# First expert's rows by one-hot products on chip, routing on turned raw rows, and one instruction section for routing and experts

## The reference

```python
h = h + g1 * (mix_x @ w_out)
t = rmsnorm(h, norm_mlp_w) * (1 + sc2) + sh2          # h is (512, 1024)
logits = t @ w_router + b_router                       # 32 experts
top_vals, top_idx = lax.top_k(logits, 4)
weights = jax.nn.softmax(top_vals)
# every expert e, on the tokens that chose it:
gate, up = jnp.split(t[rows] @ w_gu[e] + b_gu[e], 2, axis=-1)
act = (up + 1) * min(gate, 7) * sigmoid(1.702 * min(gate, 7))
y[rows] += weight * (act @ w_down[e] + b_down[e])
h = h + g2 * y
```

## Time and profile before

| what | us |
|---|---|
| median of 3 runs | 2255.71 (2254.8 to 2259.87) |
| the profiled execution's own time | 2238.22 |
| its span, first to last instruction | 2236.4 |
| PE busy | 2151.9 (96%) |
| DVE busy | 839.2 (38%) |
| ACT busy | 465.4 (21%) |
| POOL busy | 217.1 (10%) |

### The profile page before, as it was taken

The page is one execution under the profiler, slowest core; times in us unless marked ns, Lnnn a source line. Parts: engine busy times, 40 slices in busy tenths (PEclk is TensorE's granted clock), DMA queues, the critical chain, the costliest instruction groups (busy, mean ns, idle before and its releaser), DMA issues.

```text
span 2236.4 us, 34362 instructions
## 1 busy us (share of the span) xinstructions
PE 2151.9 (96%) x14207; PEld 891.3 (40%) x14207; DVE 839.2 (38%) x1585; ACT 465.4 (21%) x863; POOL 217.1 (10%) x268
## 2 busy tenths in 40 slices
PE   5999896999999999999999998999999999999998
PEld 2434542333333333333333334484445444444443
DVE  1142536823323233232332456311475022565633
ACT  2030322101111011110111012110144021654630
POOL 1000002111111111111111312000000000000000
PEclk9999997999999999999999999999999999999999
DMA  9957128999999999999999997322210221112210
GB/s 372 352 199 280 48 89 336 409 420 422 420 419 421 420 415 423 421 421 422 421 417 423 420 421 286 136 95 87 75 57 1 75 85 57 62 51 94 75 38 38
DMA packets 107105, 565.97 MB, mean 253 GB/s; under 512 B 17290, under 2 KB 29367, under 8 KB 73219
## 3 DMA queue, kind: packets, MB, share of 16 engines
q1 hardware_dynamic: 84086, 512.93, 57.0%
q0 software_dynamic: 19728, 50.02, 6.3%
q10 hardware_dynamic: 3228, 2.17, 0.3%
HBM read 545.61 MB, written 37.62 MB: 261 GB/s over the span
## 4 chain that ended last, share of the span: by engine, by line
PE 80%; DVE 2%; DMA 2%; ACT 1%; issue 0%; POOL 0%; ACTq 0%; POOLq 0%; DVEq 0%; SPq 0%
PE ps L2099 29%; PE ps L2069 10%; PE ps L379 9%; PE ps L3220 5%; PE ps L3315 5%; PE ps L3233 5%; PE ps L2077 5%; PE ps L3258 4%; PE ps L3246 2%; DMA ring<-in_w_gu 1%; PE ps L2915 1%; PE ps L2906 1%; PE ps L2615 1%; PE ps L2659 1%; PE ps L2617 1%; PE ps L2899 1%
## 5 line engine op out<-in xcount | busy, mean ns | idle before, releaser
L2099 PE MATMUL ps<-ring,xeT 128*32 128x512 f32 x6144 | 671.1, 596 | 3.7 <-DMA ring<-in_w_gu 3.3
L2099 PEld LDWEIGHTS ps<-ring,xeT 128*32 128x32 f32 x6144 | 197.2, 110 | 449.9 <-issue 445.5
L2069 PE MATMUL ps<-ring,mT 128*32 128x512 f32 x2048 | 266.5, 592 | 0.0
L1784 ACT ACTIVATE mT<-mT 128x768 f32<-128x768 f32 x32 | 27.0, 843 | 851.7 <-DVE mT L1848 851.6
L1848 DVE TENSOR_TENSOR mT<-ps,spread_bias 128x768 f32<-128x768 f32 x32 | 30.6, 957 | 435.0 <-PE ps L2099 434.9
L2077 PE MATMUL ps<-ring,mT 128*32 128x256 f32 x2048 | 157.4, 379 | 0.0
L2077 PEld LDWEIGHTS ps<-ring,mT 128*32 128x32 f32 x2048 | 66.6, 110 | 153.2 <-issue 153.2
L3220 PE MATMUL ps<-hT_late,ring 128*128 128x512 f32 x256 | 111.9, 597 | 0.5 <-issue 0.5
L3233 PE MATMUL ps<-hT_late,ring 128*128 128x512 f32 x256 | 110.5, 592 | 0.0
L379 PE MATMUL ps<-hT_late,ring 128*128 128x512 f32 x256 | 110.4, 593 | 0.0
L3315 PE MATMUL ps<-ring,mT 128*128 128x512 f32 x256 | 110.2, 592 | 0.0
(11 more groups left out here) (435 smaller groups left out, 2231.0 us busy)
## 6 DMA issues: line engine op xcount, KB each, us to landing
ring<-in_w_gu SPq DMA_DIRECT2D x128, 2048.0 KB, 10.7
ring<-in_w_down SPq DMA_DIRECT2D x128, 1024.0 KB, 11.6
y_scratch<-zeros POOLq DMA_DIRECT2D x1, 20352.0 KB, 101.3
ring<-in_even_w_in SPq DMA_DIRECT2D x18, 1024.0 KB, 9.1
ring<-in_w_ada SPq DMA_DIRECT2D x32, 512.0 KB, 9.6
ring<-in_odd_w_in SPq DMA_DIRECT2D x32, 512.0 KB, 5.4
ring<-in_w_ada SPq DMA_DIRECT2D x8, 1024.0 KB, 18.6
ring<-in_w_in SPq DMA_DIRECT2D x8, 1024.0 KB, 20.6
```

The source lines that it names most:

```text
L2069: mm = nc.tensor.matmul(quad(b, 2 * q + n), acted(k, q, src), w[:, kk, n * BANK:(n + 1) * BANK], start=first, stop=last)
L2099: mm = nc.tensor.matmul(quad(q, c), left(q), part_columns(w, c), start=start, stop=stop)
```

## The change

The normalised rows `xnt` and their modulated turned copy are no longer made for the routing. PE turns the raw rows `res` as soon as each half is added (its wait is now `res_ready`, half by half), and ACT and DVE copy four turned tiles each in one instruction (`turned`). The scale moves into the router's weights: POOL multiplies `w_router` by it once (`w_scaled`). The shift becomes one row of 32 numbers that PE works out once (`shift`, `shifts`) and DVE adds to the bias; the reciprocal root multiplies the logits (`scalar_tensor_tensor` in `logits`). In PE's list `turn(3)` goes ahead of the ranks of blocks 0 to 2, and on DVE the last steps are reordered.

Expert 0's rows are made on chip. DVE writes `first_sel`, for each token block a 128 by 96 one-hot of expert 0's places times the reciprocal root, and PE multiplies the raw rows by it: for each of 8 k-tiles, four products of 128 by 128 (every second column of `res`) and 128 by 96, added in PSUM. ACT scales and shifts out of PSUM into `xeT`. The gather of expert 0, its transposing and the three rounds of row numbers stay in the program. Round 0 of the row numbers on PE comes behind all these products, rounds 1 and 2 come behind k-steps 1 and 5 of expert 0's gate and up product, and the turning of the biases behind k-step 3.

The end of the routing section and the start of the expert section are gone as a meeting of all engines. SP waits for the last `member_ready` in its place, and no longer for the first gather. The diff without changes of indentation, cut to its core:

```diff
             def _(pool):
                 posm_zero.on(nc.gpsimd.memset(posm[:], 0.0))
+                pool.wait_ge(stream.ready[slot], landed)
+                w_scaled_ready.on(nc.gpsimd.tensor_tensor(w_scaled, w_raw, mod2[:, KD:, 0:1].to_broadcast([P, KD, E]), ALU.mult))
...
-                    for k in range(4):
-                        ins = nc.scalar.activation(hT2[:, k, t * P:(t + 1) * P], ps[:, j.bank, k * P:(k + 1) * P], ACT.Identity,
-                                                   bias=mod2[:, k, 0:1], scale=mod2[:, KD + k, 0:1])
-                    j.empty(ins)
+                    j.empty(nc.scalar.activation(hT2[:, 0:4, t * P:(t + 1) * P], bank(j.bank).rearrange("p (k n) -> p k n", k=4),
+                                                 ACT.Copy))
...
-                    xn2_ready.on(nc.vector.tensor_scalar(xnt[:, t, :], res[:, t, :], at, None, ALU.mult))
...
+                    j.empty(nc.vector.tensor_copy(hT2[:, 4:KD, t * P:(t + 1) * P], bank(j.bank).rearrange("p (k n) -> p k n", k=4)))
...
+                    n2_mean.wait(dve)
+                    j.empty(nc.vector.scalar_tensor_tensor(out=logit[:, t, :], in0=ps[:, j.bank, t * E:(t + 1) * E],
+                                                           scalar=stat[:, 4 + t:5 + t], in1=brb, op0=ALU.mult, op1=ALU.add))
...
                 output(3)
                 logits(2)
-                choose(2)
-                normalise(3)
-                modulate(3)
+                pick(2)
+                turned(3)
+                mean(3)
+                mark_members(2)
                 router_part(3)
+                inverse(3)
                 logits(3)
                 choose(3)
...
                 def turn(t):
-                    pe.wait_ge(xn2_ready.sem, t + 1)
                     for b, j in enumerate(j_h2[t]):
+                        pe.wait_ge(res_ready.sem, 2 * t + b + 1)
...
+                def shift():
+                    j_shift.open(pe)
+                    for k in range(KD):
+                        mm = nc.tensor.matmul(ps[QUAD * (k % 4):QUAD * (k % 4 + 1), j_shift.bank, NT * E:NT * E + 2], w_router[:, k, :],
+                                              mod2[:, k, :], start=k < 4, stop=k >= 4)
+                    j_shift.done(mm)
...
                 logits(2)
+                turn(3)
                 pe.wait_ge(route.sem, 2)
                 j_rank.open(pe)
                 for t in range(3):
                     ranks(t)
-                turn(3)
                 router_part(3)
...
-        with nc.Block() as block:
             @block.sync
             def _(sp):
+                member_ready.wait(sp)
                 bgu_loaded.on(sp.dma_start(bgu, A["b_gu"][0]), 16)
...
-                sp.wait_ge(M.gathered, 48)
...
-                act.wait_ge(M.xT_done, 1)
-                act_modulate(act, M)
+                for j in range(KD):
+                    act.wait_ge(first_turned.sem, rows_turned + min(j // 3 * 3 + 3, KD))
+                    nc.scalar.activation(xeT[:, j, 0:CAP], first_rows(j), ACT.Identity,
+                                         bias=modx[:, j:j + 1], scale=modx[:, KD + j:KD + j + 1]).then_inc(M.xeT_read, 1)
...
+                j_rank.emptied_for(dve)
+                for t in range(NT):
+                    first_chosen.on(nc.vector.tensor_scalar(first_sel[:, t, :], places, posm[:, t, 0:1],
+                                                            stat[:, 4 + t:5 + t], ALU.is_equal, ALU.mult))
                 split_places(list_step, posm[:, :, 0:2], place[:, :, 0:2], third_of[:, :, 0:2])
...
-                for e in range(3):
-                    pe.wait_ge(M.onehot_ready, e + 1)
...
+                first_chosen.wait(pe)
+                for j in range(KD):
...
+                    at = j // 2 * 2 * P + j % 2
+                    for t in range(NT):
+                        mm = nc.tensor.matmul(first_rows(j), res[:, t, at:at + 2 * P - 1:2],
+                                              first_sel[:, t, :], start=t == 0, stop=t == NT - 1)
+                    first_turned.on(mm)
...
+                        if first and k in (1, 5):
+                            own_ids(1 + k // 4)
+                        if first and k == 3:
+                            turn_biases()
...
+                own_ids(0)
                 block_step(0, 0, 0, True, opening=True)
```

More of the change, by code:

```diff
@@ L1407, in _ @@
                 w_router = take(pe)
+                shift()
+                w_scaled_ready.wait(pe)
                 router_part(0)
                 output(2, range(4))
+                shifts()
                 logits(0)
@@ L1650, in build @@
-        j_dw = [psum.job(i, "act") for i in range(6)]
-        def dft_product(i, dc, fw):
-            for s in range(2):
-                at, g = (s, i) if i < 4 else (2 + 2 * (i - 4) + s, 2 * (i - 4) + s)
-                for kk in range(2):
-                    mm = nc.tensor.matmul(ps[:, i, s * 256:(s + 1) * 256], dc[:, kk, at * P:(at + 1) * P],
-                                          fw[:, 2 * g + kk, :], start=kk == 0, stop=kk == 1)
-            j_dw[i].done(mm)
-        second, third = slice(E, 2 * E), slice(2 * E, 3 * E)
@@ new lines, in sum_rows @@
+            def sum_rows(dve, n0, n1):
+                for n in range(n0, n1):
+                    i, t = divmod(n - NT * TOPK, NT)
+                    w = w_end[:, i, t:t + 1] if i >= 0 else w_early[:, n:n + 1]
+                    if i < 0:
+                        t = n // TOPK
+                    dve.wait_ge(rowed[n % GB].sem, 16 * (n // GB + 1))
+                    if n:
+                        row_used.wait(dve)
+                    row_used.on(nc.vector.scalar_tensor_tensor(out=res[:, t, :], in0=gbuf[n % GB], scalar=w, in1=res[:, t, :],
+                                                               op0=ALU.mult, op1=ALU.add))
@@ new lines, in pass_on @@
+            def pass_on(pool, S, n):
+                pool.wait_ge(S.marked, n)
+                nc.gpsimd.tensor_tensor(mark[:], ident[:, 0:1], ident[:, 0:1], ALU.mult).then_inc(S.marked, 1)
+            M = Expert(*[sem(f"moe_{name}") if name not in ("up_done", "sel_ready") else None for name in EXPERT_SIGNALS])
+            buffers_zero = amat_zero.n + 2
+            consts = {}
+            bgu_loaded = signal("bgu_loaded")
+            bias_turned = signal("bias_turned")
+            first_chosen, first_turned = Signal(rms_sum.sem), Signal(rms_root.sem)
@@ L1662, in _ @@
+            second, third = slice(E, 2 * E), slice(2 * E, 3 * E)
             @block.sync
             def _(sp):
+                member_ready.wait(sp)
                 bgu_loaded.on(sp.dma_start(bgu, A["b_gu"][0]), 16)
```

416 lines of the change are left out of this document (221 added, 195 removed).

## The result

The changed kernel takes 2261.96 us (median of 15 runs, 2259.94 to 2266.13), the kernel before 2257.67 in the 15 runs beside it: a ratio of 1.0020, 95% interval 1.0013 to 1.0027, so 4.3 us slower. The forecast was 3.6 us slower. The difference stands just under the 4.5 us that I had called the least to tell from no change; with 15 runs of each kernel the interval leaves no change out.

A forecast was written before the change was run, and what follows sets the result against it. PE bounds the expert train, so the start of expert 1's gate and up product (387.03 us) decides. It moves to 388.7, 1.7 later; the fallen clock adds 1.9: 3.6 us slower, 2259.3 us, range 2251 to 2266.

The forecast's parts named there:

- The front: PE's list ahead of the last output product: 9 small products for the shift add 0.6 us (0.3 to 1.0).
- Block 3's tail and the meeting: End of routing: places at 343.6, 3.2 us earlier; without the engines' meeting between sections, the products start at 345.1.
- The products: Expert 0's rows on PE: 64 passes, half slow, half at 0.096 us, 9.4 us in all, ending at 354.5.
- the rival of slow products: Passes for expert 0's rows cost 0.22 us throughout, 14 us in all; sum 8.3 us slower, 2264.0; chance 0.25.
- my own three signs of being wrong: Gather landing within 3 us, DVE having the biases before PE ends expert 0's product, or passes averaging over 0.16 us.
- The gather: Expert 0's gather, still waited for by DVE: last issue at 358.9, landing 8.5 us later, at 367.4, beside weight loads.
- VectorE's chain: DVE from transposing expert 0's gather to scaled biases: 19.1 us, half of the 2.92 exponential wait taken off; biases at 386.6.
- TensorE's pause: PE, ready at about 377.3, pauses 11 us ahead of expert 1's product, for third row numbers, then biases.
- The clock: Clock falls in PE's pause; expert 1's product runs at half clock from 388.7 to 392.5, losing 1.9 us (0 to 2.9).
- The sum: Whole kernel: expert 1's product 1.7 us later, with the clock 3.6 us slower, 2259.3 us, 0.16% more; chance 0.52.
- The quick gather: Expert 0's gather lands 2.7 us after issue, so expert 1 starts at 382.9; 5 us faster, 2250.7; chance 0.18.
- The stream as pace of the opening: Weight loads, not PE, decide; loads issued 12 us earlier bring up to 8 us, 2247.7; chance 0.05.

The follow-up runs named there:

- no_first_gather: Changed kernel without the gather of expert 0 and its transposing on VectorE, round 0 of the row numbers kept; 2254.41 us, ratio 0.9981 to the kernel before.
- loads_after_gather: Changed kernel with SyncE issuing the last three pairs of gate and up weights only once expert 0's gather has landed; 2254.81 us, ratio 0.9990 to the kernel before.
- the routing part alone: Kernel before with only the diff's routing part, two sections and expert 0 by its gather as before; 2261.60 us, ratio 1.0015.
- the second profile of the kernel before: Kernel before, unchanged, profiled once more; 2259.75 us in its one run.
- routing_alone_loads_held: Kernel before with only the routing part, SyncE's two routing-section weight loads held until block 3's row store landed; 2263.73 us, ratio 1.0028.

## Why the prediction was right

*The mechanism.* Each step is in the trace: places earlier, products slow then fast, the gather late, VectorE's chain last, TensorE's pause, the clock. `no_first_gather` and `loads_after_gather` show, by taking away the gather or what makes it late, that the late gather makes the difference between 4 us slower and 4 us faster.

*The front.* The last output product ends 62.92 us from the mark instead of 62.06: 0.86 for `shift` and `shifts`, 0.6 said.

*Block 3's tail and the meeting.* The places come 72.20 from the mark (75.08 before, as 346.80 less its mark 271.72), 2.9 earlier, 3.2 said. The step was wrong on one point all the same. It took the meeting for worth 1.4 us, and the store on GpSimd for free. The store landed only 10.3 us after its issue, at 355.9, and with two sections the meeting would have waited for it: the routing part alone is 3.3 us slower. The earlier places count only because the meeting is gone. With one section the statement holds: GpSimd is free at 357.0, the row numbers come at 360.

*The products.* This is the term that was mis-sized: 11.4 us (348.17 to 359.56), 9.4 said. I took 96/128 of the price of 128 columns; a pass costs 0.222 and 0.125 us, near the full price (0.246 and 0.128). With a rise after 5.9 us that alone makes 11.0; the rise after 6.9 us is the rest. The mean pass of 0.17 lies beyond the 0.16 from which I had put the rival of slow products, so one of my own three signs of being wrong was met; the rival's reason, the step of two columns, is not what did it. By the Trainium skill, Advanced Engine Details and Errata, section SBUF Cachelines, such reads run at full rate; 3.81 against 4.01 us agrees to 5%.

*The gather.* The last issue came 2.3 us later than said (89.5 from the mark, 87.2 said), because the products ended later; to landing 8.75 us, 8.5 said. The Trainium skill, DMA: Bandwidth & Descriptors, section on the anatomy of one DMA, would give 2.3 us by estimate: that agrees with the 2.1 of `loads_after_gather`, and is a quarter of what the gather takes beside the loads.

*VectorE's chain.* From the transposing to the biases' end, 372.64 to 390.66, 18.0 us, 19.1 said: the wait for the exponential is 0.28, none of its 2.92 is left, and I had taken half. That gave back 1.1 of the products' 2.0 and kept the sum near 4 us. That the two misses pull against each other is luck.

*TensorE's pause.* 7.2 us, 11 said. TensorE was through 109.0 us from the mark, 105.6 said: the products ended 2 us later, and from there to the end of expert 0's product, with what had moved into it, it took 23.8 us, 22.5 said. VectorE bounded all the same, so this moved nothing.

*The clock.* It fell 2.5 us into the pause; I had said 2.4, which in the kernel before is 2.1 when counted from TensorE's last product there (333.99, not 333.78). The half product lost 1.42, 1.9 said. The biases took 0.95 longer, but from `wT` to expert 1's product it is 2.56 us against 2.07 before, so 0.5 of that reached the start.

*The sum.* By these rows 4.4 us against the second profile of the kernel before and 4.9 against the first, 3.6 said, 4.3 measured.

*The rivals.* The quick gather is out as the kernel stands (8.75 us), and is what `loads_after_gather` makes true, 3.5 us faster; I had put it at 5. The stream as pace of the opening is out by the same run.

## What to carry to other kernels

Before work is moved off a transfer, look whether the transfer is still made and who still waits for it: here TensorE got its rows without the gather, and the kernel got slower, because VectorE's queue still had the wait for it. When an instruction that releases a buffer is moved, follow the load that it lets go, and list the small transfers that are on the way at that time; here a store, a gather or a bias issued behind weight loads landed 4.4 to 13.8 us after its issue, where stores and gathers with none beside them took 2.1 to 3.0. Holding the weights back paid where nothing waited for the small transfers behind them (`loads_after_gather`) and cost where TensorE did (`routing_alone_loads_held`). Part of a change can lose by itself: the routing part alone, from which 3 us were expected, was 3.3 us slower. Time the parts.

## What was not expected of the hardware

A store of one block's rows, 128 rows, took 2.9 us with nothing beside it, 4.4, 7.5 and 8.3 us with two weight loads issued 9.4, 8.0 and 5.5 us ahead of it, and 10.3 with the biases behind it as well. In that last case three more weight loads made no difference: it was 10.3 with them in the changed kernel and 10.2 without them in `loads_after_gather`. Passes of TensorE with 128 by 128 stationary numbers took 0.22 us at half clock and 0.125 at full with 96 moving columns, and 0.22 with 48 at half clock. The granted clock came up to 1.00 6.9 us after the products began in the changed kernel, 12.8 us in the run with the row numbers between them and 17 us in the run with the narrower products, though the rows show TensorE busy all the time; why is open. The kernel before ran an expert in 31.24 us in one execution and 31.9 in another.
